# The value products of the second mixer's attention turned round, two heads at a time

## The reference, cut to what matters

```
o = g[...,0:1]*o_cmp + g[...,1:2]*o_sel + g[...,2:3]*o_win
```

## Time and profile before

| | us |
|---|---|
| median of 3 runs | 3051.1 |
| the runs | 3051.84, 3044.52, 3051.1 |
| span of the profiled execution | 3046.4 |
| PE busy | 2894.0 (95%) |
| PE load busy | 2372.3 (78%) |
| DVE busy | 2035.4 (67%) |
| ACT busy | 1166.6 (38%) |
| L1435 PE, 1056 records | 143.2 |

### The profile page before, as it was taken

How to read it: one execution, slowest core, us unless ns; L and a number is a source line. 1 busy time by engine, 2 the same in 40 slices (tenths; PEclk the granted TensorE clock), 3 DMA queues, 4 the chain that set the end, 5 groups by cost and what they waited for, 6 DMA issues and landing times.

```text
span 3046.4 us, 39610 instructions
## 1 busy us (share of the span) xinstructions
PE 2894.0 (95%) x15451; PEld 2372.3 (78%) x15451; DVE 2035.4 (67%) x3470; ACT 1166.6 (38%) x1969; POOL 78.3 (3%) x152
## 2 busy tenths in 40 slices
PE   3999999998998998899999999989988999999999
PEld 3868885677887888687888888868867788888887
DVE  5444316678436456558777777779985877777875
ACT  3234225643325555434333334431134433333444
POOL 1000000110030000000000000000000000000000
PEclk8999999998999999799999999999989999999999
DMA  7110200024100000223333274311101333335632
GB/s 308 29 32 22 63 23 15 1 77 130 48 19 1 1 1 1 90 98 111 111 111 111 83 260 156 98 51 49 36 16 63 104 111 111 111 111 187 219 97 102
DMA packets 185700, 256.28 MB, mean 84 GB/s; under 512 B 29575, under 2 KB 138539, under 8 KB 181035
## 3 DMA queue, kind: packets, MB, share of 16 engines
q1 hardware_dynamic: 181520, 232.45, 22.9%
q10 hardware_dynamic: 3995, 21.30, 1.7%
HBM read 186.62 MB, written 67.11 MB: 83 GB/s over the span
## 4 chain that ended last, share of the span: by engine, by line
PE 67%; DVE 8%; ACT 1%; issue 1%; DMA 0%; DVEq 0%; ACTq 0%
PE ps L1532 26%; PE ps L1540 14%; PE ps L1487 10%; PE ps L1435 3%; PE ps L1345 3%; PE ps L1417 2%; PE ps L1399 2%; PE ps L1596 2%; PE ps L1096 1%; PE ps L1647 1%; PE ps L975 1%; DVE ht L2814 0%; PE ps L1323 0%; PE ps L1393 0%; DMA ring<-in_ffn_w_gate_dram 0%
## 5 line engine op out<-in xcount | busy, mean ns | idle before, releaser
L1532 PE MATMUL ps<-x_ops,w_ring 128*128 128x512 f32 x3696 | 840.3, 389 | 6.2 <-DVE even_rows L2962 3.1
L1532 PEld LDWEIGHTS ps<-x_ops,w_ring 128*128 128x128 f32 x3696 | 693.2, 188 | 151.4 <-issue 7.8
L1540 PE MATMUL ps<-a_ring,w_ring 128*128 128x512 f32 x1848 | 419.5, 389 | 0.0
L1540 PEld LDWEIGHTS ps<-a_ring,w_ring 128*128 128x128 f32 x1848 | 346.7, 188 | 72.4 <-DVE w_ring L2903 0.5
L1487 PE MATMUL ps<-h_high,ring_parts 128*128 128x512 f32 x1024 | 319.7, 394 | 18.2 <-DVE h_low L2381 9.3
L2099 ACT ACTIVATE w_ring<-ring 128x512 fp32r<-128x512 f32 x230 | 144.4, 630 | 300.3 <-PE ps L1532 284.5
L1487 PEld LDWEIGHTS ps<-h_high,ring_parts 128*128 128x128 f32 x1024 | 193.1, 190 | 64.4 <-issue 13.6
L2390 DVE TENSOR_TENSOR ring_parts<-ring,ring_parts 128x1024 fp32r<-128x1024 f32 (+2 forms) x77 | 91.7, 1191 | 209.6 <-ACT ring_parts L1734 209.0
L1487 PE MATMUL ps<-h_low,ring_parts 128*128 128x512 f32 x512 | 200.7, 392 | 0.0
L2903 DVE TENSOR_TENSOR w_ring<-ring,w_ring 128x512 fp32r<-128x512 f32 x230 | 158.0, 687 | 38.8 <-ACT w_ring L2099 38.8
L1734 ACT ACTIVATE ring_parts<-ring 128x1024 fp32r<-128x1024 f32 (+2 forms) x77 | 76.0, 990 | 275.3 <-PE ps L1487 177.1
(11 more groups left out here) (471 smaller groups left out, 4729.9 us busy)
## 6 DMA issues: line engine op xcount, KB each, us to landing
a_raw<-act_kept SPq DMA_DIRECT2D x70, 512.0 KB, 3.7
act_kept<-even_rows SPq DMA_DIRECT2D x12, 1536.0 KB, 5.1
act_kept<-odd_rows SPq DMA_DIRECT2D x10, 1536.0 KB, 5.1
ring<-in_ffn_w_gate_dram SPq DMA_DIRECT2D x12, 1024.0 KB, 5.6
ring<-in_ffn_w_up_dram SPq DMA_DIRECT2D x12, 1024.0 KB, 5.9
ring<-in_conv_w_pw_dram SPq DMA_DIRECT2D x24, 512.0 KB, 3.9
late<-in_ffn_w_gate_dram SPq DMA_DIRECT2D x10, 1024.0 KB, 5.6
late<-in_ffn_w_up_dram SPq DMA_DIRECT2D x10, 1024.0 KB, 6.1
```

Of the source, the lines that this page charges most:

```text
L1532: last = mm(o, w_ring[:, i % 4, wp_, P * k:P * k + P], x_ops[:, X_OP[p], rp_, k, :], start=p in "176" and k == 0 and p_ == 0, stop=k == 3 ...
L1540: last = mm(bank(OUT_BANK[DOWN_GROUP[p] + c_]), w_ring[:, (A_UNITS + b) % 4, wp_, P * c_:P * c_ + P], a_ring[:, b % 4, rp_, :], start=p in ...
```

## The change

The stationary and the moving operand of the win and sel value products change places: the values (128 keys x 64) are stationary and the turned weights (128 keys x 128 queries) move. Two heads, the even one and the odd one behind it, are computed together, one product of each in turn: the even head on columns 0 to 63 of the array, the odd on 64 to 127. The output then has the head dimension on partitions, two heads for each 128 columns; ScalarE copies it out for 4 heads (`out_taken`), and TensorE turns it back by two transposes (`turned_out`) before VectorE's `n_outs`. The column of ones is gone: the denominator is now accumulated by the exponential (`accum_out`). `pt` has eight slots instead of four. The steps behind are moved: pairs at step 3 behind the odd head, turned_out 5, n_outs 6 behind (cmp of group 0 still 4), n_heads 8. The selection of each group is cut into three parts at win h = 1, 2, 4 and h = 5, 6, 7, and stands after `n_outs`. `o_taken` becomes two counters, one for each group. In the first mixer six semaphores become three, with the same waits.

```diff
         nin_root = sc[:, 0, :]
         crow = flat_ht[:, 2112:2624].rearrange("p (g n) -> p g n", g=2)
         oacc = flat_ht[:, 2624:3648].rearrange("p (i n) -> p i n", i=2)
-        pt = sc[:, 2:4, :].rearrange("p a b -> p (a b)")
+        pt = sc[:, :, :].rearrange("p a b -> p (a b)")
+        out_t = flat_ht[:, 1056:1568].rearrange("p (g n) -> p g n", g=2)
+        row_sums = misc[:, 64:80]
         root_sum, root_col = misc[:, 272:280], misc[:, 280:288]
         x_square_sums, x_1_sums = misc[:, 264:272], misc[:, 256:264]
...
-        s.o_taken = sem("o_taken")
+        s.o_turned_in = sem("o_turned_in")
+        s.o_turned = sem("o_turned")
+        o_taken = [sem("o_taken0"), sem("o_taken1")]
...
-            for step in range(len(units) + 8):
+            for step in range(len(units) + 10):
                 if 0 <= step - 2 < len(units):
                     units[step - 2].turn = turns
                     turns += len(units[step - 2].pieces)
-                if step - 6 in last_of:
+                if step - 8 in last_of:
                     turn_of.append(turns)
...
-            def n_values(un):
-
-                o = bank(6 + un.g)
-                if un.first and un.o + un.br:
-                    pe.wait_ge(s.o_taken, 2 * (3 * un.o + un.br - 1) + un.g + 1)
-                for m, (a, blocks) in enumerate(un.pieces):
-                    pe.wait_ge(s.n_copied, un.turn + m + 1)
-                    for b in range(blocks):
-                        weights = pt[:, 512 * ((un.piece + m) % 4) + P * b:512 * ((un.piece + m) % 4) + P * b + P]
-                        if un.kind == "cmp":
-                            last = mm(o[:, P * b:P * b + P], weights, vb[:, un.g, :], start=b == 0, stop=True,
-                                      skip_group_check=True)
-                        else:
-                            r, at = un.h % 4, a + b
-                            last = mm(o[:, 65 * r:65 * r + 65], weights, (vw, vs)[un.br - 1][:, un.b0 + at, un.g, :],
-                                      start=r == 0 and at == 0, stop=at == un.blocks - 1, skip_group_check=True)
-                    last.then_inc(s.n_summed, 1)
+            def out_free(un):
+
+                if un.o + un.br:
+                    pe.wait_ge(o_taken[un.g], 3 * un.o + un.br)
+                return bank(6 + un.g)
+
+            def piece_of(un, b):
+
+                p_ = un.piece + b // 4
+                return pt[:, 512 * (p_ % 8) + P * (b % 4):512 * (p_ % 8) + P * (b % 4) + P]
+
+            def c_values(un):
+
+                o = out_free(un)
+                pe.wait_ge(s.n_copied, un.turn + 1)
+                for b in range(2):
+                    last = mm(o[:, P * b:P * b + P], piece_of(un, b), vb[:, un.g, :], start=b == 0, stop=True,
+                              skip_group_check=True)
+                last.then_inc(s.n_summed, 1)
+
+            def pair_values(left_, right_):
+
+                o = out_free(left_) if left_.first else bank(6 + left_.g)
+                c_ = left_.h % 4 // 2
+                pe.wait_ge(s.n_copied, right_.turn + len(right_.pieces))
+                for b in range(left_.blocks):
+                    for half, un in enumerate((left_, right_)):
+                        last = mm(o[64 * half:64 * half + 64, P * c_:P * c_ + P],
+                                  (vw, vs)[un.br - 1][:, un.b0 + b, un.g, 0:N_D], piece_of(un, b),
+                                  start=c_ == 0 and b == 0, stop=b == left_.blocks - 1, skip_group_check=True)
+                last.then_inc(s.n_summed, len(left_.pieces) + len(right_.pieces))
+
+            def turned_out(un):
+
+                pe.wait_ge(s.o_turned_in, 4 * un.o + 2 * (un.br - 1) + un.g + 1)
+                for c_ in range(2):
+                    o = 3072 + 512 * un.g + 256 + P * c_
+                    last = pe.transpose(ps[:, o:o + P], out_t[:, un.g, P * c_:P * c_ + P], ident[:, :])
+                last.then_inc(s.o_turned, 1)
...
-            for step in range(N_NSA + 6):
+            at = lambda n, kind: 0 <= n < N_NSA and (nsa_units[n].kind == "cmp") == (kind == "cmp")
+            for step in range(N_NSA + 9):
                 if step < N_NSA:
                     n_scores(nsa_units[step])
                 if 0 <= step - 2 < N_NSA:
                     n_turns(nsa_units[step - 2])
-                if 0 <= step - 3 < N_NSA:
-                    n_values(nsa_units[step - 3])
-                if step - 6 in nsa_last:
-                    n_heads(nsa_last.index(step - 6))
+                if at(step - 3, "cmp") and nsa_units[step - 3].g == 0:
+                    c_values(nsa_units[step - 3])
+                if at(step - 5, "cmp") and nsa_units[step - 5].g == 1:
+                    c_values(nsa_units[step - 5])
+                if at(step - 3, "soft") and nsa_units[step - 3].h % 2:
+                    pair_values(nsa_units[step - 4], nsa_units[step - 3])
+                if at(step - 5, "soft") and nsa_units[step - 5].last:
+                    turned_out(nsa_units[step - 5])
+                if step - 8 in nsa_last:
+                    n_heads(nsa_last.index(step - 8))
...
-                    f(row, row, ACT.Exp, bias=r[:, 0:1], scale=-1.0).then_inc(s.n_exp, 1)
+                    f(row, row, ACT.Exp, bias=r[:, 0:1], scale=-1.0,
+                      accum_out=row_sums[:, un.row % 16:un.row % 16 + 1]).then_inc(s.n_exp, 1)
 
             def n_copies(un):
 
                 for m, (_, blocks) in enumerate(un.pieces):
                     t, p_ = un.turn + m, un.piece + m
                     a.wait_ge(s.n_turned, t + 1)
-                    if p_ >= 4:
-                        a.wait_ge(s.n_summed, p_ - 3)
-                    f(pt[:, 512 * (p_ % 4):512 * (p_ % 4) + P * blocks],
+                    if p_ >= 8:
+                        a.wait_ge(s.n_summed, p_ - 7)
+                    f(pt[:, 512 * (p_ % 8):512 * (p_ % 8) + P * blocks],
                       ps[:, 2048 + 512 * (t % 2):2048 + 512 * (t % 2) + P * blocks], ACT.Copy).then_inc(s.n_copied, 1)
 
-            for step in range(N_NSA + 6):
+            def out_taken(un):
+
+                a.wait_ge(s.n_summed, un.piece + len(un.pieces))
+                f(out_t[:, un.g, :], bank(6 + un.g)[:, 0:256], ACT.Copy).then_inc(s.o_turned_in, 1)
+
+            for step in range(N_NSA + 9):
                 if step < N_NSA:
                     n_exps(nsa_units[step])
                 if step == N_NSA:
                     a.dma_start(xt[:, :, :], x_kept).then_inc(s.x_back, 16)
+                if 0 <= step - 4 < N_NSA and nsa_units[step - 4].kind != "cmp" and nsa_units[step - 4].last:
+                    out_taken(nsa_units[step - 4])
                 if 0 <= step - 2 < N_NSA:
                     n_copies(nsa_units[step - 2])
-                if step - 6 in nsa_last:
-                    i = nsa_last.index(step - 6)
+                if step - 8 in nsa_last:
+                    i = nsa_last.index(step - 8)
...
-            def selection(i, g):
+            def selection(i, g, part_):
...
+                if part_ == 0:
+                    chain(v.tensor_reduce(i0, pp[:, 4:68].rearrange("p (j n) -> p j n", n=4)[:, :, 0:3], AX.X, add))
+                    chain(tt(i1, pp[:, 7:68:4], pp[:, 3:64:4], add))
+                    chain(stt(i0, i1, 0.5, i0, mul, add))
+                elif part_ == 1:
+                    chain(tt(i0, i0, force[:, i, :], add))
+                    chain(v.max(top[:, 0:8], i0))
+                    chain(v.match_replace(rep, top[:, 0:8], i0, -BIGF))
+
+                    chain(ts(rep, rep, -2e38, NEG, ALU.is_gt, mul))
+                else:
+                    nb = 2 * (i + 1)
+                    chain(tt(tg[:, g, 0:w].rearrange("p (b n) -> p b n", b=nb),
+                             causal[:, P * (7 - i):P * (7 - i) + w].rearrange("p (b n) -> p b n", b=nb),
+                             rep[:, 0:nb].unsqueeze(2).to_broadcast([P, nb, 64]), add))
...
-            v.memset(vs[:, :, :, N_D:N_D + 1], 1.0)
-            v.memset(vw[:, :, :, N_D:N_D + 1], 1.0)
...
-                v.wait_ge(s.n_summed, un.piece + len(un.pieces))
                 o = oacc[:, un.o % 2, 256 * un.g:256 * un.g + 256].rearrange("p (r d) -> p r d", r=4)
                 gate = ng[:, un.i, 12 * un.g + (0, 2, 1)[un.br]:12 * un.g + 12:3]
                 src = bank(6 + un.g)
                 if un.kind == "cmp":
+                    v.wait_ge(s.n_summed, un.piece + 1)
                     if un.o >= 2:
                         v.wait_ge(s.n_turned, nsa_turn[un.o - 2] + 1)
                     tt(o, src[:, 0:256].rearrange("p (r d) -> p r d", r=4), gate.unsqueeze(2).to_broadcast([P, 4, N_D]),
-                       mul).then_inc(s.o_taken, 1)
+                       mul).then_inc(o_taken[un.g], 1)
                 else:
-                    d = den[:, 2 + un.g, :]
-                    src = src[:, 0:260].rearrange("p (r n) -> p r n", r=4)
-                    chain(v.reciprocal(d, src[:, :, N_D]))
```

(71 more changed lines are left out.)

## The result

The changed kernel takes 3060.7 us (median of 16 runs), the kernel before 3051.7 in the same rounds: a ratio of 1.0034 (95% interval 1.0025 to 1.0043), some 10 us slower. The forecast was 3062 us.

The account below looks back on a forecast made before the run. Bound: the loop over four engines, level with TensorE nearly everywhere. Slower pairs +20.4, output copy and turning back +16, last outputs +1, heads -26.4 make +11 us; 3051.1 + 11 = 3062 us, range 2998 to 3092.

Parts of the forecast that it names:

- the loop: Attention stage: two consecutive steps can't be shorter than scores, bias, exponential, copy plus TensorE's work behind that copy; 0.58.
- The first rival: Stage: TensorE is the bound after all, so work taken off it counts: -55 us, 2996; chance 0.15.
- both limits: Stage: the loop over four engines and TensorE's own work, said to be level nearly everywhere.
- Pairs: Two steps, both heads' values in one: 5 blocks 5.30 us (before 4.84), 8 blocks 7.30 (7.17), 3 blocks 3.27 (3.01).
- V: Value products of a pair of heads on TensorE: 0.213 us per block plus 0.37, halves fully overlapped; 1.44 for 5 blocks.
- the chain: From a unit's scores on TensorE until it may use ScalarE's copy: 5 blocks 3.2 us, plus 0.09 for the accumulator read.
- Output copy and turning back: ScalarE's output copy, 0.27 us, and TensorE's two transposes, 0.23, neither with cover: 32 x 0.5 = +16 us.
- Accumulator read: Reading the exponential's accumulated sums on ScalarE adds 0.09 us to the chain, in each of 64 pairs.
- Heads: Steps k0 to k9 of each row block: later outputs and three-part selection end the L1431 stop, -26.4 us over the stage.
- Side by side: Value products on the two column halves: taken to overlap fully; the rival without overlap +56 us, 3118, chance 0.04.
- The drain at a change of mode: TensorE drains when the tiling mode changes, two switches for each of 64 pairs: 64 x 0.3 = 19 us.
- The rival: The clock falls because TensorE idles 1.3 us in each pair: +45 us, 3107; chance 0.08.

Follow-up runs that it names:

- The opened loop: The changed kernel with ScalarE's copies of the turned pieces ahead of the new unit's exponential, not after it: 2994.9 us, ratio 0.9822.
- the added work: Transposes done twice in win and sel steps without value products: 3058.0 us in the changed kernel, 3013.6 us in the changed kernel with ScalarE's copies first.
- longer bursts: The changed kernel with all value products of the even head, then all of the odd head, instead of in turn: 3093.7 us, ratio 1.0141.
- the copy alone: The changed kernel with ScalarE's copy of the four heads' output moved behind the copies of the turned pieces in the same step: 3052.9 us, ratio 1.0004.

## Why the prediction was right

- **What bounds the stage.** Right: the loop of scores, bias, exponential and copy, with what TensorE does behind the copy. The opened loop (65 us), the added work (nothing in one kernel, 16 us in the other) and the 0.70 us of longer bursts that showed up as 0.71 in the pair show it three ways. The first rival, TensorE as the bound, falls with them: the work went (39 us of busy time in the stage) and the span didn't follow. Where the prediction says that both limits are equal nearly everywhere, it goes too far: for 2 and 3 blocks TensorE's own work lay 0.3 to 0.45 us below the loop.
- **Pairs.** 5 blocks: forecast 5.30, measured 5.24 (i = 4), 5.36 in the timeline above. 8 blocks: 7.30, measured 7.27. 3 blocks: 3.27, measured 3.19. Terms inside were off against each other: in the timeline above V for 5 blocks is 1.25, not 1.44, while the transposes ahead of it take 0.66 us, not 0.57, and the chain 3.45, not 3.29. How much of V's 0.37 is the switches no run shows.
- **Output copy and turning back.** Forecast 0.5 us each. Pairs that hold one take 5.73 where the next takes 5.24; the copy alone measured 9 us in 32.
- **Accumulator read.** Forecast 64 x 0.09; measured 6 us.
- **Heads.** Forecast: k0 to k9 of i = 6 from 32.4 to 29.2 us; measured 30.67. Over the eight row blocks the heads went from 204.6 to 201.0 us, 4 less, where the sum had some 9 less (-26.4, and in each of eight heads the 2.2 charged for slower pairs and output turns). So -26.4 should have been about -21: the term is over-sized by 5 us. The heads of i = 5, 1 and 0 grew, by 0.7, 0.3 and 0.9 us, where I had a small gain. The later steps (k10 on, with the tail) took 17.4 us more; the same reckoning leaves 20. Within them the stretch behind the last scores went from 6.9 to 9.1 us, where the sum had +1.
- **The total.** 3062 against 3060.7 is closer than the parts deserve. The gain of the heads was taken 5 us too large, the pairs of up to 4 blocks 0.1 us too dear each (32 of them, some +0.15 measured and +0.26 forecast). These errors went against each other, and that the total came within 2 us is luck. What the runs bear out is the loop, and its terms to within 5 us. The stated range (2998 to 3092) was wide enough to hold a gain as well.
- **Side by side.** Right: 20 passes in 1.25 us, 1.95 when the heads follow one another. Two passes in turn take 0.125 us, one behind the other 0.195: the overlap is large, not full.
- **The drain at a change of mode**, which I weighed from the Trainium skill (TensorEngine Tiling (Array Packing), Key Properties): TensorE's weight loads show it as 0.17 us of "issue" ahead of each burst and again behind it, and over the stage 40 such waits with 19.2 us in all ahead of L1449:

```profile
939.09 1.07 PEld L1449 LDWEIGHTS ps<-sc,big 128*64 128x64 f32 x20 [0.17 <-issue]
...
940.34 0.76 PEld L1400 LDWEIGHTS ps<-kt,qt 128*128 128x128 f32 x4 [0.17 <-issue]
```

  That total holds waits for other things too (the longest is 1.5 us); with the loop open it is 48 waits and 8.6 us, the longest 0.3. The trace agrees with the rule, at about 0.17 us a switch. Its price in the span was not measured by itself: no run here has half columns without the switch.
- **The clock.** The rival did not come: the mean over the stage is 0.92, before 0.90, and in the later steps of i = 7 to 1 it is 1.00, the upper level, with an idle of 1.3 us in each wide pair. But the head's term took for granted that the fall of the clock behind L1431 goes, and in part it stayed: the heads of i = 6, 5, 3 and 1 stand at 0.94, 0.89, 0.93 and 0.83, before at 0.89, 0.89, 0.87 and 0.83. With the added transposes these four heads are at 1.00 and together 8.2 us shorter, so the clock fits as the reason why the term was over-sized; no run shows it alone.

## What to carry to other kernels

An engine that is busy 95% of the time can still be level with a loop over other engines; before work is taken from it, add up the loop from the start of one instruction to the next use of its result, and see whether that sum is as long. Where it is, the order inside another engine's program (here a copy behind an exponential that it doesn't need) is worth more than the work: 21 us in the kernel before and 65 in the changed one, for moving two lines. And a change with several parts should be timed part by part: this one held 13 us of gain and more than that of loss.

## What was not expected

- Adding 28 us of transposes made the kernel no slower and rather faster (1.0023 against 1.0034, intervals that overlap). All of the gain in the profiles is in the heads. In the head of i = 5 TensorE stands 1.98 us ahead of L1468, the four transposes behind a row block (to 1052.14), and the clock is 0.74 from 1054 to 1058 us; with the added transposes it stands 1.43 us there and the whole head is at 1.00. Over all runs the core's mean clock is 0.973 (median of 12) against 0.970 (median of 16). That the work kept the clock up fits; what sets the level off is not shown.
- The swing by opening the loop in the narrow blocks of the kernel before, 0.3 to 0.45 us in two steps, where TensorE's marked gaps were at most 0.35 us (2 blocks) and for 3 blocks none.
- Passes on one half of the columns cost 0.098 us one behind the other and 0.107 by the prediction's reckoning in the first mixer; in turn on both halves 0.06 each.
